# Attention of a two-layer trunk: the long probability tile turned by DMA, narrow value products, gating shared by ScalarE and GpSimd

## The reference

```python
def odd_layer(x, cos, sin, norm_g, w_in, q_lat_g, w_uq, kv_lat_g, w_ukv, q_head_g, k_head_g, w_out):
    h = rms_norm(x, norm_g)
    c_q, c_kv, k_rope, z = jnp.split(h @ w_in, [...], axis=-1)
    q = (rms_norm(c_q, q_lat_g) @ w_uq).reshape(B, S, MLA_HEADS, QK_HEAD)       # 16 heads of 96
    kv = (rms_norm(c_kv, kv_lat_g) @ w_ukv).reshape(B, S, MLA_HEADS, QK_NOPE + V_HEAD)
    ...
    q = rope_tail(rms_norm(q, q_head_g), cos, sin)
    k = rope_tail(rms_norm(k, k_head_g), cos, sin)
    o = causal_attention(q, k, v)          # softmax(q k^T / sqrt(96), causal) v, v of 64 columns a head
    return x + (o * jax.nn.silu(z)) @ w_out
```

## Time and profile before

| | |
|---|---|
| time, median of 3 runs | 963.06 us (962.77 to 963.10) |
| profiled execution, its own time | 963.16 us |
| span from the first to the last instruction in it | 961.3 us |
| mean granted clock of TensorE over the span | 0.998 of full speed |
| busy: TensorE, VectorE, ScalarE, GpSimd | 946.9, 813.6, 579.6, 376.2 us |
| attention stage | about 656 to 882 us of the span |

### The profile page before, as it was taken

One profiled execution on the slowest core, in us unless ns is written; L12 is line 12 of the kernel. 1 busy time (PEld: TensorE's weight loads), 2 busy tenths in 40 slices (PEclk: granted clock), 3 DMA queues, 4 the chain that ended last, 5 costly groups with the idle time before them and its releaser, 6 DMA issues.

```text
span 961.3 us, 16137 instructions
## 1 busy us (share of the span) xinstructions
PE 946.9 (98%) x5830; PEld 668.8 (70%) x5830; DVE 813.6 (85%) x1410; ACT 579.6 (60%) x1076; POOL 376.2 (39%) x425
## 2 busy tenths in 40 slices
PE   9999999999999999999999999999999999999998
PEld 7788544444688887644457999898778877887443
DVE  5798899899865579989787899988999999998763
ACT  7434544434434454454646888867999999998230
POOL 0002243222000002235412577857773589897220
PEclk9999999999999999999999999999999999999999
DMA  9320431111055422432023264566565766460231
GB/s 306 46 58 23 110 83 50 44 45 45 1 178 166 137 66 66 119 101 67 21 72 110 93 208 161 185 181 176 116 170 142 169 154 114 94 170 2 88 110 66
DMA packets 165343, 103.67 MB, mean 108 GB/s; under 512 B 75272, under 2 KB 149520, under 8 KB 165008
## 3 DMA queue, kind: packets, MB, share of 16 engines
q1 hardware_dynamic: 159216, 102.25, 37.8%
q10 hardware_dynamic: 6048, 0.39, 0.5%
HBM read 56.48 MB, written 29.36 MB: 89 GB/s over the span
## 4 chain that ended last, share of the span: by engine, by line
PE 79%; DVE 12%; POOL 3%; issue 3%; ACT 3%; POOLq 0%; DVEq 0%; ACTq 0%
PE banks L111 23%; PE banks L113 22%; PE banks L112 22%; PE banks L2732 5%; PE banks L2750 2%; PE banks L2751 1%; DVE front_lt L1223 1%; ACT front_set_b L723 1%; DVE heads_probs_big L2490 1%; DVE front_l L1223 1%; DVE front_w_row L1065 1%; ACT heads_probs_big L2352 1%; PE banks L2759 1%; DVE heads_pt_lo L2498 1%; DVE front_set_b L1082 1%
## 5 line engine op out<-in xcount | busy, mean ns | idle before, releaser
L2498 DVE TENSOR_TENSOR heads_pt_lo<-banks,heads_pt_hi 128x512 f16<-128x512 f32 (+2 forms) x192 | 102.1, 554 | 11.2 <-ACT heads_pt_hi L2361 7.0
L2361 ACT ACTIVATE heads_pt_hi<-banks 128x512 f16<-128x512 f32 (+2 forms) x192 | 88.4, 485 | 4.9 <-PE banks L2732 4.6
L2750 PE MATMUL banks<-heads_v,heads_pt_hi 128*128 128x128 f16 x576 | 74.5, 220 | 0.0
L2732 PE MATMUL banks<-ident,heads_probs_big 128*128 128x128 f32 x416 | 69.1, 279 | 1.4 <-ACT heads_probs_big L2352 1.3
L2751 PE MATMUL banks<-heads_v,heads_pt_lo 128*128 128x64 f16 x576 | 69.5, 193 | 0.0
L2490 DVE CUSTOM_DVE_ANT_0 heads_probs_big<-banks,heads_mask,score_scale 128x1024 f32<-128x1024 f32 (+1 forms) x64 | 68.5, 1071 | 0.9
L2352 ACT ACTIVATE heads_probs_big<-heads_probs_big,heads_neg_max 128x1024 f32<-128x1024 f32 (+1 forms) x64 | 63.4, 991 | 5.6 <-DVE heads_neg_max L2490 3.6
L111 PE MATMUL banks<-front_act_hi,front_w_hi 128*128 128x512 f32 x160 | 63.9, 399 | 0.3 <-DVE front_w_lo L943 0.3
L111 PE MATMUL banks<-heads_k_t,heads_q_t 96*128 96x512 f16 (+2 forms) x192 | 62.9, 327 | 0.9 <-DVE heads_neg_max L2490 0.9
L113 PE MATMUL banks<-front_act_hi,front_w_lo 128*128 128x512 f32 x160 | 62.4, 390 | 0.0
L112 PE MATMUL banks<-front_act_lo,front_w_hi 128*128 128x512 f32 x160 | 62.3, 389 | 0.0
(11 more groups left out here) (488 smaller groups left out, 3099.3 us busy)
## 6 DMA issues: line engine op xcount, KB each, us to landing
qk_scratch<-heads_y SPq DMA_DIRECT2D x22, 512.0 KB, 3.6
front_x<-in_x_t SPq DMA_DIRECT2D x16, 512.0 KB, 5.4
front_raw<-in_w_in_ab SPq DMA_DIRECT2D x14, 512.0 KB, 5.2
qk_scratch<-heads_last_y SPq DMA_DIRECT2D x10, 512.0 KB, 3.5
front_w<-in_w_out_ab SPq DMA_DIRECT2D x8, 512.0 KB, 3.8
x_scratch<-front_x SPq DMA_DIRECT2D x8, 512.0 KB, 4.0
v_scratch<-heads_v SPq DMA_DIRECT2D x32, 128.0 KB, 3.0
heads_v_st<-v_scratch SPq DMA_DIRECT2D x8, 512.0 KB, 5.1
```

What stands on the lines that cost most here:

```text
L2361: nc.scalar.activation(pt_hi[:, q % PIECES, :width], t_ps[:, banks[("piece", n, k)] % 3, :width], ACT.Copy).then_inc(pt_high, 1)
L2498: nc.vector.tensor_tensor(pt_lo[:, q % PIECES, :width], t_ps[:, banks[("piece", n, k)] % 3, :width], pt_hi[:, q % PIECES, :width], ALU.sub ...
L2732: last = nc.tensor.transpose(t_ps[:, b, r * P:(r + 1) * P], probs(n, j * P, (j + 1) * P), ident[:])
L2750: nc.tensor.matmul(out, pt_hi[:, q % PIECES, blk], v2[e][:, j, :], start=(j == 0), stop=False)
```

## The change

1. *The longest tile.* In heads 1 to 15 the first row tile (`by_queue`) is no longer turned by TensorE. ScalarE casts the 1024 columns of probabilities in SBUF to their high part (`big_high`), VectorE makes the low part (`big_low`), and SyncE turns both with a DMA transpose each (`turn_big`), SBUF to SBUF, in its queue behind the keys and queries of the next head. Its value product (`big_product`) comes seven steps later (`BIG_BEHIND`) in place of two, and so the group it belongs to is copied out and scaled three steps later.
2. *The value products* are three matmuls of 64 columns a block, all onto the same 64 columns of PSUM. The copy out of PSUM halves its width, and GpSimd's sum of the two halves goes.
3. *The gating* of pairs 0 to 6 is a copy out of PSUM by ScalarE (`take_out`) and a product on GpSimd (`pool_gating`), which stands between the two scalings of each even head. The last pair stays as it was.
4. *Around it:* the norms are spread at unit 26 in place of 24 and the exponential's table is fetched at unit 28 in place of 27; the ring of turned pieces has five places in place of six; GpSimd's own chains wait on one common semaphore; sums of weights, residual rows and values lie in other places in SBUF, the residual rows are loaded once all scores are there, and the maximum over the second pair's weights waits for the sums that now overwrite a part of them.

The diff, cut to its core:

```diff
@@ -1706,24 +1706,29 @@
...
+        res_at = (ring_at, ring_at + 3 * tile, ring_at + tile, ring_at + 2 * tile)
+        self.v_at = spare + 10 * 1024
+        self.big = [at(name, [P, NK, P], F16, place) for name, place in (
+            ("big", spare + 10 * 1024), ("big_lo", w_place + GROUP_W * 4 + 10 * 1024))]
+        self.big_t = [at(name, [P, NK, P], F16, place) for name, place in (
+            ("big_t", spare + 12 * 1024), ("big_t_lo", spare))]
+        self.big_high, self.big_low, self.big_done, self.big_in = sem("big_high"), sem("big_low"), sem("big_done"), sem("big_in")
...
@@ -1836,21 +1839,18 @@
...
-    def pool_plain(self, pool, m):
+    def pool_plain(self, pool, link, m):
         hi, lo, raw = self.plain_hl[m][:, 0], self.plain_hl[m][:, 1], self.plain_raw[m][:]
...
         pool.wait_ge(self.w_in[m], 32)
-        self.nc.gpsimd.tensor_scalar(raw, raw, self.plain_scale, None, ALU.mult).then_inc(self.plain_scaled, 1)
-        pool.wait_ge(self.plain_scaled, m + 1)
-        self.nc.gpsimd.tensor_copy(hi, raw).then_inc(self.plain_high, 1)
-        pool.wait_ge(self.plain_high, self.split_base + m + 1)
+        link(self.nc.gpsimd.tensor_scalar(raw, raw, self.plain_scale, None, ALU.mult))
+        link(self.nc.gpsimd.tensor_copy(hi, raw))
         self.nc.gpsimd.tensor_tensor(lo, raw, hi, ALU.subtract).then_inc(self.plain_done, 1)
-    def pool_gate(self, pool, k):
+    def pool_gate(self, pool, link, k):
         hi, lo, raw = self.gate_hl[k][:, 0], self.gate_hl[k][:, 1], self.gate[:, k, :]
         pool.wait_ge(self.gated, 2 * k + 2)
-        self.nc.gpsimd.tensor_copy(hi, raw).then_inc(self.gate_cast, 1)
-        pool.wait_ge(self.gate_cast, k + 1)
+        link(self.nc.gpsimd.tensor_copy(hi, raw))
         self.nc.gpsimd.tensor_tensor(lo, raw, hi, ALU.subtract).then_inc(self.gate_done, 1)
...
@@ -1918,8 +1916,8 @@
...
             dve.wait_ge(self.w_in[m + n], 32)
-        if q == 0:
-            dve.wait_ge(self.joint.s_added, 4 * ALL_PAIRS + 4)
+        if q < 2:
+            dve.wait_ge(self.joint.s_added, 4 * (ALL_PAIRS + q) + 4)
         self.nc.vector.tensor_reduce(self.w_row[:, q:q + 1], self.w[:, m:m + 2].rearrange("p m k c -> p (m k c)"),
...
@@ -2030,7 +2028,7 @@
...
     LATE, LATE_LOW = UNITS - 4, UNITS - 6
-    AHEAD, BEHIND, TURN_LAG, PIECES = 2, 2, 5, 6
+    AHEAD, BEHIND, TURN_LAG, PIECES, BIG_BEHIND = 2, 2, 5, 5, 7
     ROOT_STEP = 3
...
@@ -2083,9 +2081,9 @@
-    o_at = lat_hi_at + PIECES * BANK * 4
-    o_raw = at("o_raw", [P, 2, 4, 2 * VH], F32, o_at)
-    o_sum = at("o_sum", [P, 2, 4, VH], F32, o_at + 16 * VH * 4)
+    o_at = lat_hi_at + 12 * 1024
+    o_raw = at("o_raw", [P, 2, 4, VH], F32, o_at)
+    turned_out = at("turned_out", [P, 2, BANK], F32, o_at + 8 * VH * 4)
@@ -2109,7 +2107,7 @@
...
     v_high, v_low = sem("v_high"), sem("v_low")
-    o_copied, o_summed, o_scaled = sem("o_copied"), sem("o_summed"), sem("o_scaled")
+    o_copied, o_scaled, o_taken = sem("o_copied"), sem("o_scaled"), sem("o_taken")
     o_turned, gated, mask_set = sem("o_turned"), out.gated, sem("mask_set")
...
@@ -2179,12 +2177,21 @@
...
-    PER_HEAD = sum(len(pieces(i)) for i in range(NT))
+    def by_queue(n):
+        return n > 0 and n % NT == 0
+    def parts(n):
+        return [] if by_queue(n) else pieces(tile_of(n)[1])
+    piece_base = [0]
+    for n in range(N):
+        piece_base.append(piece_base[-1] + len(parts(n)))
...
-        h, p = divmod(n, NT)
-        return PER_HEAD * h + sum(len(pieces(ORDER[x])) for x in range(p)) + k
+        return piece_base[n] + k
...
@@ -2193,19 +2200,19 @@
...
-                    banks[n_banks] = (gated, 2 * pair + c + 1)
+                    banks[n_banks] = (gated if pair == PAIRS - 1 else o_taken, 2 * pair + c + 1)
-    NORMS, NORM_UNIT, EXP_UNIT = (4, 7, 8, 9, 11, 15, 16, 17, 19, 23), 24, 27
+    NORMS, NORM_UNIT, EXP_UNIT = (4, 7, 8, 9, 11, 15, 16, 17, 19, 23), 26, 28
@@ -2271,6 +2278,14 @@
...
             sp.dma_start(v_st[:], by_tile(v_d)[:, :, h * VH:(h + 2) * VH]).then_inc(v_in, 16)
+        def turn_big(h):
+            for part, made in enumerate((out.big_high, out.big_low)):
+                sp.wait_ge(made, h)
+                if h > 1:
+                    sp.wait_ge(out.big_done, h - 1)
+                sp.dma_start_transpose(out.big_t[part][:], out.big[part][:].rearrange("p b k -> p (b k)")
+                                       ).then_inc(out.big_in, 16)
...
@@ -2311,6 +2326,7 @@
             load_q(h)
+            turn_big(h - 1)
             if out.PLAIN <= h - HPG < NK:
...
@@ -2318,6 +2334,8 @@
...
                 store_qk(LATE_LOW + h - 2)
+        turn_big(HEADS - 1)
+        sp.wait_ge(s_ready, N)
         for m in range(out.PLACES_OF_ROWS):
...
@@ -2361,11 +2379,28 @@
...
+        def take_out(pair, c):
+            act.wait_ge(o_turned, 2 * pair + c + 1)
+            if pair:
+                act.wait_ge(gated, 2 * pair + c - 1)
+            nc.scalar.activation(turned_out[:, c], t_ps[:, banks[("turn", pair, c)] % 3, :], ACT.Copy).then_inc(o_taken, 1)
+        def big_high(n):
+            h = n // NT
+            if h == 1:
+                for e in range(VSLOTS):
+                    act.wait_ge(v_stored[e], 16 * len(range(e, UNITS, VSLOTS)))
+            act.wait_ge(exp_done, n + 1)
+            act.wait_ge(out.big_in, 32 * (h - 1))
+            nc.scalar.activation(out.big[0][:].rearrange("p b k -> p (b k)"), probs(n, 0, S), ACT.Copy).then_inc(out.big_high, 1)
         def copy_out(g):
+            if g % 2 == 0 and g:
+                act.wait_ge(out.big_done, g // 2)
             act.wait_ge(pv_done, piece_no(4 * g + 3, len(pieces(ORDER[(4 * g + 3) % NT])) - 1) + 1)
             if g >= 2:
-                act.wait_ge(o_summed, g - 1)
-            nc.scalar.activation(o_raw[:, g % 2], o_ps[:, g % 2], ACT.Copy,
+                act.wait_ge(o_scaled, g - 1)
+            nc.scalar.activation(o_raw[:, g % 2], o_ps[:, g % 2, :, :VH], ACT.Copy,
                                  scale=out.o_scale[:, g // (2 * HPG):g // (2 * HPG) + 1]).then_inc(o_copied, 1)
...
@@ -2413,12 +2448,21 @@
...
             if n < N:
-                for k in range(len(pieces(tile_of(n)[1]))):
+                for k in range(len(parts(n))):
                     high(n, k)
...
                 exponentials(n + AHEAD)
+            if by_queue(n + 1) and n + 1 < N:
+                big_high(n + 1)
+            for pair in range(PAIRS - 1):
+                for c in range(2):
+                    if n == turn_step(pair, c) + 1:
+                        take_out(pair, c)
             if n >= BEHIND and (n - BEHIND) % 4 == 3:
-                copy_out((n - BEHIND) // 4)
+                if (n - BEHIND) // 4 % 2 or n < NT:
+                    copy_out((n - BEHIND) // 4)
+            if n % NT == 0 and n > NT:
+                copy_out(2 * (n // NT) - 2)
             for w in range(LATE_LOW, UNITS):
...
@@ -2485,8 +2529,10 @@
...
             dve.wait_ge(s_ready, n + 1)
-            if n >= 4:
-                dve.wait_ge(pt_ready, piece_no(n - 4, len(pieces(tile_of(n - 4)[1])) - 1) + 1)
+            if n >= 4 and by_queue(n - 4):
+                dve.wait_ge(out.big_low, (n - 4) // NT)
+            elif n >= 4:
+                dve.wait_ge(pt_ready, piece_base[n - 3])
             nc.vector.tensor_tensor_reduce(probs(n, 0, width), scores(i, 0, width), mask[:, S - width:],
...
@@ -2498,6 +2544,13 @@
...
+        def big_low(n):
+            h = n // NT
+            dve.wait_ge(out.big_high, h)
+            dve.wait_ge(out.big_in, 32 * (h - 1))
+            nc.vector.tensor_tensor(out.big[1][:].rearrange("p b k -> p (b k)"), probs(n, 0, S),
+                                    out.big[0][:].rearrange("p b k -> p (b k)"), ALU.subtract).then_inc(out.big_low, 1)
         def inverse(g):
...
@@ -2508,6 +2561,7 @@
...
             dve.wait_ge(o_turned, 2 * pair + c + 1)
+            dve.wait_ge(gated, 2 * pair + c)
             nc.vector.tensor_tensor(g, g, t_ps[:, banks[("turn", pair, c)] % 3, :], ALU.mult).then_inc(gated, 1)
...
@@ -2542,15 +2596,16 @@
...
-                for k in range(len(pieces(tile_of(n)[1]))):
+                for k in range(len(parts(n))):
                     low(n, k)
+                if by_queue(n):
+                    big_low(n)
                 if n % 4 == 3:
...
             last_root(n)
-            for pair in range(PAIRS):
-                for c in range(2):
-                    if n == turn_step(pair, c):
-                        gating(pair, c)
+            for c in range(2):
+                if n == turn_step(PAIRS - 1, c):
+                    gating(PAIRS - 1, c)
             if n == N:
...
@@ -2640,17 +2695,19 @@
...
             pair, e = h // 2, h % 2
-            raw = o_raw[:, g % 2]
             pool.wait_ge(o_copied, g + 1)
-            nc.gpsimd.tensor_tensor(o_sum[:, g % 2], raw[:, :, :VH], raw[:, :, VH:], ALU.add).then_inc(o_summed, 1)
-            pool.wait_ge(o_summed, g + 1)
             pool.wait_ge(inv_done, g + 1)
```

(52 more changed lines are left out.)

36 lines of the change are left out of this document (15 added, 21 removed).

## The result

The changed kernel takes **973.82 us** (median of 4 runs, 973.42 to 974.54), the kernel before 963.08 (962.77 to 963.39): ratio 1.0111, interval 1.0099 to 1.0124. It is 1.1% slower. I had forecast 964.6 with a range of 953 to 970; the time lies outside it. (One of the ten executions of the later run e12 took 1378 us, at a mean granted clock of 0.655; its ratio leaves it out.) The span grew from 961.3 to 971.7 us.

A forecast was written before the change was run, and what follows sets the result against it. It took TensorE as the bound, ScalarE and VectorE close behind, GpSimd without slack at pair 6. Terms −3 (to head 8's keys), +4.2 (to pair 6's turn), +0.3 (tail) gave +1.5 on 963.16: 964.6 us, range 953 to 970.

The forecast's parts named there:

- my 107: Keys' issue of head 8 to turn of pair 6: time in us if TensorE and ScalarE alone set the pace.
- TensorE, products 0: Value products: three 64-column matmuls a block cost −2 to +3 us over 576 blocks, taken as 0.
- ScalarE +0.2 a head: Attention heads: ScalarE's copies removed, added and narrowed come to +0.2 us a head, so ScalarE sets the pace.
- The late values: SyncE's queue: values wait behind the long tile's transposes, landing 16.2 us after the keys' issue; GpSimd's stretch starts 4.4 later.
- The lock, +7.7: Heads 8 to pair 6's turn: VectorE's low part holds the shared SBUF port, lengthening GpSimd's work 1.1 us a head.
- GpSimd's stretch, +4.2: Keys' issue of head 8 to turn of pair 6: GpSimd's work and late values give 115.1 us against 110.9.
- The norm, −1: Stretch before the heads: moving the norm's matmul removes TensorE's wait and slow clock, −1 us (bounds −4 and 0).
- The tail, +0.3: After the turn of pair 6: −0.9 for the last long tile, −0.3 for the last scaling, +1.5 for the clock.
- R3: Rival: each DMA transpose holds SyncE 4 us, values and turned tiles come later, +5 + 4, 973 us; chance 0.12.
- R4: Rival: the third weight load binds in the value products, 0.02 us a block, half of 12 us, 970; chance 0.06.
- R1: Rival: the lock and late values don't bind GpSimd, 955 us; half-way form 960 to 961; chance 0.36 with it.
- R2: Rival: only TensorE counts, 13 us of transposes and 4 of the norm go, 946 to 950 us; chance 0.05.

The follow-up runs named there:

- e12: The changed kernel with the long tile turned by TensorE again and ScalarE's copy of a turned half first in its step: 961.93 us, ratio 0.9986.
- e16: The changed kernel with VectorE's low part of the long tile made for only 8 of 1024 columns from head 2 on: 972.00 us.
- e1: The changed kernel with the long tile's product one step later, eight behind its tile in place of seven: 969.36 us.
- e17: The changed kernel with ScalarE's copy of a turned half first in its step, ahead of the exponential: 971.73 us.
- e18: e7 with ScalarE's copy of a turned half first in its step: 962.59 us, ratio to the kernel before 0.9997.
- e5: The changed kernel with parts 1 and 3 undone (long tile back on TensorE, gating back on VectorE): 962.05 us.
- e7: e1 with the load of the values ahead of the long tile's DMA transposes in SyncE's queue: 965.64 us.
- e8: The changed kernel with the long tile's product one step later, the gating back on VectorE and the values first in SyncE's queue: 962.27 us.
- e11: e8 with VectorE's low part of the long tile made for only 8 of 1024 columns from head 2 on: 960.51 us.
- e14: e8 with the long tile's product four steps behind its tile and its group's copy at the old step: 976.65 us.
- e15: e8 with the long tile's product five steps behind its tile and its group's copy at the old step: 973.78 us.
- e10: e8 with the turns of the pairs two steps later, lag 7 for 5: 966.58 us.
- e4: The changed kernel with the low part a VectorE cast of the probabilities alone, the subtraction left out: 971.25 us.

## Why the prediction was wrong

The step that failed is "TensorE and ScalarE alone, at 0.5 less for each of eight heads, would have come to 107". From the keys' load of head 8 to the turn of pair 6 the changed kernel took 118.03 us (last window above). In it TensorE waited for GpSimd once, at that turn:

```profile
875.49 0.63 PE L2832 MATMUL banks<-ident,heads_o_pair 128*128 128x128 f32 x4 [1.22 <-POOL heads_o_pair L2702]
```

So without that one wait TensorE, VectorE and ScalarE would have taken 116.8, 10 us more than my 107; the lock's share in VectorE's low parts is in it, and the whole of the low parts is worth 1.8 us of the kernel (e16). I had worked out each engine's total and let the largest set the pace, less 0.2 for unevenness. In the kernel before TensorE was busy for whole windows, so that the order in the other queues was covered. With 0.87 us a head taken off TensorE, the round from scores to maxima to exponential to transposes sets the pace, as I read these waits, and what counts is where an instruction stands in it. The product stood ahead of the scores of the third tile (e1), ScalarE's copy behind an exponential (e12, e17, e18).

The three terms of my sum were −3 up to the keys' load of head 8, +4.2 from there to the turn of pair 6, and +0.3 behind it. They measured +1.8 (757.46 against 755.65), +7.1 and +1.5. In the first and the second the heads were to be shorter by the engines' totals, and they were longer.

Point by point:

- *TensorE, products 0*: right. In the changed kernel three blocks take from 785.78 to 786.04, 0.087 us each, against 0.085; e5 shows no cost.
- *ScalarE +0.2 a head*: its copies took 1.04, 0.58 and 0.46 where I had put 1.15, 0.67 and 0.47. In the two heads from 814.93 to 843.13 it was busy 13.03 and 12.10, mean 12.57, as before. The totals were right enough and the conclusion from them wrong. (That three engines were within 5% of each other is true of the head without a turn alone: in the other ScalarE had 12.58 of 14.00, 10% less.) With the order mended the totals come nearer: two heads of e18 take 12.96 and 13.66, mean 13.31, against the 13.0 that my 12.8 and 0.2 give.
- *The late values*: right. I had 16.2 us from the keys' load to the split; it was 773.63 − 757.46 = 16.17, with the low part's end at 8.8 us for my 8.5 and the queue free at 10.1 for my 10. What they cost is in e7 and e8, 3.7 and 1.3 us. In the changed kernel GpSimd waited for values three times from 757.5 to 875.5 (the view of waits: us in total, times, longest):

```profile
POOL heads_v L2691 <- DMA heads_v_st<-v_scratch: 7.2, 3, 4.1
```

- *The lock, +7.7*: mis-sized. The low part was lengthened in five late heads (0.28, 1.20, 0.53, 0.67 and 1.07 us) and not at all in three others. GpSimd was busy 93.1 us from that split to that turn; 94.7 − 3.6 = 91.1 without any lock, so some 2 us by this estimate, where I had 98.8. A full GpSimd doesn't meet every low part, and e16 and e11 put VectorE's part and the lock together at 1.8.
- *GpSimd's stretch, +4.2*: its sign was right, 118.03 against 110.9, and the chain that ended last does run as I had it at the end, from the long tile's DMA transpose through the load of the values into GpSimd's work, up to the turn at 875.49. The chain's pieces at its start (start, us, what):

```profile
824.47 1.23 SPq L2287
825.70 0.05 issue
825.75 4.24 DMA heads_v_st<-v_scratch
```

 But it ended only 1.22 us behind everything else that the turn needs, where I had expected some 8 us for the four turns, so that GpSimd set the time by that much and not by 8. In its 101.9 us of wall time from the split to the turn it was busy 93.1. Of my signs of being right, the waits for the values came; a wait of 5 us at the turn, a clock under 1 behind it, and ScalarE busy over 97% of heads 3 to 5 (it was 90 to 94%) did not.
- *The norm, −1*: TensorE's stall and the slow clock went, as the window of the unit stage in the changed kernel shows against rows 12:

```profile
608.00:633.20 25.20, 25.20 (x138) 23.84 (x137) 24.39 (x51) 18.01 (x38) 18.83 (x25) 1.00 0.36 131
```

 But VectorE is busy 24.39 in both, and the keys' load of head 4 comes at 700.17 in this run, and in e5, which has the same move, at 701.28 against 701.42. So the gain is near my bound of nothing.
- *The tail, +0.3*: from the turn of pair 6 to the end it was 96.21 us against 94.76, +1.5; the other 1.8 of the +3.2 above lie ahead of it, since the turn comes 17.5 us after the keys' load of head 15 in place of 15.7, the wait of 1.22 in it. What makes the +1.5 I didn't follow. The slow clock that I had priced at 1.5 didn't come: behind the wait of 1.22 the granted clock was 1.00 from 875.49 to 900.
- *R3* gave 973, near the measured time, for a reason that didn't hold. SyncE's source row of the long tile's transposes:

```profile
L2287 SPq DMA_TRANSPOSE out_big_t<-out_big x15: 1232/1232/1579, 680.1 to 879.4; - x15
...
DMA to landing us min/median/max: 3.0/3.1/4.3
```

 1.23 us to issue, 3.1 to land, cheaper than the 1.5 of my own sum, and in the changed kernel TensorE never waited for them. *R4* is refuted by e5. *R1* and *R2* would have needed the round to shrink with the engines' totals, and it grew.

Two of my later theories fell too. I called it two halves, TensorE's up to the third tile's scores and ScalarE's behind them, and expected from it that any work moved into TensorE's idle gaps was free. e14 and e15 show that it isn't, and e10 that moving the turns out of the first half gains nothing. What stands is narrower: of the four steps tried for the product, the one behind the third tile's scores gave the shortest round. Why exactly the round is 12.9 us there, and what of it would move next, stays open; ScalarE's 12.1 busy of 12.9 leaves little.

No version beats the kernel before by more than a measurement can tell apart easily: e12 is 0.14% under it, e5, e8 and e18 the same as it.

## What to carry to other kernels

When several engines are within a few per cent of each other, taking work off the one that never waits doesn't shorten the loop by that work: the order in all queues, covered until then, becomes the bound. So before forecasting from totals, walk one period step by step and write down for each moved instruction what stands directly behind it on its engine and who waits for that. A late, independent product did best here right behind the instruction that others wait for (e1), and a copy that frees a bank did best ahead of one that can wait (e12, e17, e18); a gap in an engine's timeline is not room if what it waits for depends on the work that follows the gap.

## What the runs showed of the hardware that I had not expected

- The port lock also catches a VectorE cast with a single SBUF operand: 2.64 us for one of 0.69 beside a GpSimd instruction of 2.13 (e4). By the Trainium skill ("SBUF — State Buffer", SBUF: two separate sides) the holders are VectorE's operations in a 2-port mode, and those with two SBUF inputs against a GpSimd instruction that reads SBUF. This cast's 0.69 us for 1024 columns, against 1.22 with two inputs, fits such a mode, though no run here shows the mode itself.
- The lock costs both sides: in e10 VectorE's instruction ran 1.7 us longer (2.94 for 1.22) and GpSimd's next one 1.0 longer (1.60 for 0.62).
- A matmul of 64 columns with a weight load of its own starts every 0.029 us in the long tile's product: 24 of them took 0.70 us (789.68 to 790.37 in the changed kernel).
- A DMA transpose from SBUF to SBUF of 128 x 1024 float16 took 1.23 us to issue and 3.1 to land, less than that of the keys from DRAM, which SyncE issued in 1.8 to 3.0 us.
